# A mixture-of-experts job table: a shorter VectorE chain, work moved to ScalarE and GpSimd, first weights ahead of the gathers, half the filler products

## The reference

```
logits = h @ w_router + b_router
top_vals, top_idx = top_k(logits, 4)             # 32 experts
gates = softmax(top_vals)
for each expert e and each of its tokens t:
    hid = h[t] @ w1[e] + b1[e]                   # 1024 x 2048
    y   = clamped_swiglu(hid) @ w2[e] + b2[e]    # 1024 x 1024
    out[t] += gate * y
```

## Time and profile before

| what | us |
|---|---|
| median of 3 runs (lowest, highest) | 1971.47 (1968.91, 1974.28) |
| the profiled execution | 1971.53 |
| its span, first to last instruction | 1969.7 |
| TensorE busy | 1910.2 (97%) |
| weight loading of TensorE busy | 1398.8 (71%) |
| VectorE / ScalarE / GpSimd busy | 1303.0 / 411.8 / 235.6 |
| mean granted TensorE clock | 0.989 |
| moved by DMA | 498.39 MB, 253 GB/s on the mean |

### The profile page before, as it was taken

One profiled execution on the slowest core, in us unless ns is written; L12 is line 12 of the kernel. 1 busy time (PEld: TensorE's weight loads), 2 busy tenths in 40 slices (PEclk: granted clock), 3 DMA queues, 4 the chain that ended last, 5 costly groups with the idle time before them and its releaser, 6 DMA issues.

```text
span 1969.7 us, 33296 instructions
## 1 busy us (share of the span) xinstructions
PE 1910.2 (97%) x12224; PEld 1398.8 (71%) x12224; DVE 1303.0 (66%) x3759; ACT 411.8 (21%) x910; POOL 235.6 (12%) x317
## 2 busy tenths in 40 slices
PE   7999999997999999999999999999998999999996
PEld 5677777774999999999999999834333444444442
DVE  2787778774377777775666666645355767777665
ACT  1233332222121122222222222223221100001100
POOL 1212222221010111111111111110100000000000
PEclk8999999998999999999999999999999999999998
DMA  9411100113966778788888989999999999999992
GB/s 311 113 43 43 43 18 35 32 33 144 339 207 228 246 261 269 245 282 278 289 285 283 307 300 304 316 368 381 360 368 382 382 375 356 369 369 367 360 360 72
DMA packets 207682, 498.39 MB, mean 253 GB/s; under 512 B 7716, under 2 KB 14928, under 8 KB 200080
## 3 DMA queue, kind: packets, MB, share of 16 engines
q1 hardware_dynamic: 194016, 449.43, 63.7%
q0 software_dynamic: 11312, 39.85, 8.2%
q10 hardware_dynamic: 2304, 8.39, 1.0%
HBM read 470.24 MB, written 27.41 MB: 253 GB/s over the span
## 4 chain that ended last, share of the span: by engine, by line
issue 40%; PE 29%; DMA 5%; POOL 1%; DVE 1%; POOLq 0%; ACT 0%; DVEq 0%; ACTq 0%
PE ps_unit L1885 29%; DMA out_dram<-y_rows,idx_cur 4%; POOL x_got L1378 1%; DMA x_got<-h_rows,idx_next 0%; PE ps_list L1857 0%; POOL carrier L1374 0%; POOL out_dram L1435 0%; POOLq L1096 0%; POOLq L1290 0%; DVE match L1562 0%; DVE reached L1610 0%; POOL out_dram L1390 0%; POOLq L1426 0%; POOLq L1265 0%; DVE xT L1684 0%
## 5 line engine op out<-in xcount | busy, mean ns | idle before, releaser
L1885 PE MATMUL ps_unit<-xT,w_slot 128*128 128x136 f32 (+6 forms) x3840 | 521.5, 298 | 1.6 <-DVE xT L1684 1.6
L1885 PEld LDWEIGHTS ps_unit<-xT,w_slot 128*128 128x128 f32 x3840 | 516.6, 196 | 2.0 <-issue 2.0
L1915 PE MATMUL ps_unit<-w_slot,xT 128*128 128x512 f32 x704 | 306.7, 594 | 0.0
L1279 DVE STREAM_TRANSPOSE xT<-x_got 32x256 f32<-32x256 f32 x644 | 280.5, 436 | 12.1 <-DMA x_got<-h_rows,idx_next 3.7
L1885 PE MATMUL ps_unit<-act_T,w_slot 128*128 128x136 f32 (+6 forms) x1920 | 261.6, 298 | 0.1
L1885 PEld LDWEIGHTS ps_unit<-act_T,w_slot 128*128 128x128 f32 x1920 | 257.9, 190 | 2.2 <-DVE act_T L1659 1.5
L1915 PEld LDWEIGHTS ps_unit<-w_slot,xT 128*128 128x128 f32 x704 | 132.8, 190 | 163.0 <-issue 163.0
L1675 DVE STREAM_TRANSPOSE y_rows<-yT 32x256 f32<-32x256 f32 x372 | 162.1, 436 | 55.0 <-ACT yT L1481 50.1
L928 PE MATMUL ps_c<-hT,w_in_sb 128*128 128x128 f32 x1536 | 182.1, 279 | 4.3 <-DMA w_in_sb<-in_w_in_dram 4.3
L928 PEld LDWEIGHTS ps_c<-hT,w_in_sb 128*128 128x128 f32 x1536 | 177.3, 194 | 9.6 <-DMA w_in_sb<-in_w_in_dram 5.2
L1374 POOL TENSOR_TENSOR carrier<-carrier 128x1 f32<-128x1 f32 x64 | 14.5, 227 | 1319.1 <-issue 610.8
(11 more groups left out here) (294 smaller groups left out, 1790.5 us busy)
## 6 DMA issues: line engine op xcount, KB each, us to landing
w_slot<-in_w_dram SPq DMA_DIRECT2D x192, 2048.0 KB, 12.1
b_row<-in_b_dram SPq DMA_DIRECT2D x11, 1024.0 KB, 12.9
w_in_sb<-in_w_in_dram SPq DMA_DIRECT2D x6, 1024.0 KB, 12.0
b_row<-in_b_dram SPq DMA_DIRECT2D x11, 512.0 KB, 15.1
x_in<-in_x_dram SPq DMA_DIRECT2D x8, 512.0 KB, 3.5
x_res<-in_x_dram SPq DMA_DIRECT2D x8, 512.0 KB, 4.7
out_dram<-x ACTq DMA_DIRECT2D x8, 512.0 KB, 5.1
h_rows<-h ACTq DMA_DIRECT2D x8, 512.0 KB, 3.1
```

Source lines behind the costliest of these rows:

```text
L1279: last = nc.vector.transpose(out[c * Q:(c + 1) * Q, :, tokens], rows.rearrange("p (k c j) -> p k c j", c=P // Q, j=Q)[:, :, c, :])
L1885: last = pe.matmul(ps_unit[p % RING][:, u, 0:n], w, moving[:, k, 0:n], start=(k == 0), stop=(k == KD - 1))
L1915: last = pe.matmul(ps_hid[c], xT[:, k, 0:P], w_slot[:, c, k, :], start=(k == 0), stop=(k == KD - 1))
```

## The change

- VectorE's chain: `counts` is copied first and `rank` later, after the fields. `ended`, `first`, `past` (twice) and `size` are issued without a wait of their own, with independent operations put side by side. The two gate subtracts, the copies of sorted fields and the counts of jobs leave VectorE; it copies one row `ends_f` out of PSUM (a float copy of the ends), which ScalarE converts.
- ScalarE: casts and writes `ends`, `jobs`, `job_row` and `base_row`; it clears `x_got` in four parts after that.
- GpSimd: does the two gate subtracts, the first ahead of its three bias loads, the second behind them, into a buffer `gates_left` of their own; it clears `x_got` no longer and waits for the four parts before the gathers.
- TensorE: ranks and counts go to the bank of `ps_act`, and the five filler products behind them to `ps_list`. The permutation waits for `ends_taken` in place of three table entries. The whole table is awaited ahead of the first list, and four filler products stand between the register loads in place of eight.
- SP: waits for three table entries and the experts' row, loads one register, issues the first piece of weights, waits for both gathers, and issues the other five pieces. The wide loop starts at the second job, and `job_counts` comes behind it.

The declarations of the new buffer and semaphores are left out of the diff.

```diff
         ps_list = ps("ps_list", [P, 512])
         ps_act = ps("ps_act", [P, 4, P])
         ps_x = ps_unit[2:]
+        ps_ranks = ps_act[:].rearrange("p k q -> p (k q)")
...
-        TABLES = 6
+        TABLES = 5
...
 
             sp.wait_ge(pool_moved.sem, 32)
             sp.wait_ge(rows_moved.sem, 16)
-            wide, slim_jobs, narrow_jobs, full = job_counts(sp)
+            sp.wait_ge(experts_read, 1)
+            sp.wait_ge(table_ready, TABLES - 2)
+            wide = sp.value_load(ends[0:1, last_size - 1:last_size], min_val=0, max_val=most_jobs)
             with sp.If(wide > 0):
-                with sp.Fori(0, wide) as q:
+                e = expert_of(sp, 0)
+                load_pieces(0, bass.ds(e, 1))
+                wait(sp, gathered_a, 0)
+                wait(sp, gathered_b, 0)
+                for i in range(1, LOADS):
+                    load_pieces(i, bass.ds(e, 1))
+            with sp.If(wide > 1):
+                with sp.Fori(1, wide) as q:
                     e = expert_of(sp, q)
                     for i in range(LOADS):
                         wait(sp, w_used[i], q - 1)
                         load_pieces(i, bass.ds(e, 1))
+            _, slim_jobs, narrow_jobs, full = job_counts(sp)
             with sp.If(slim_jobs > 0):
                 with sp.Fori(0, slim_jobs) as s:
                     q = s + wide
...
         def _(pool):
+            pool.wait_ge(parts_cast[0], 1)
+            nc.gpsimd.tensor_tensor(gates_left[:], gates[:], gate_parts[:, :, 0, :], ALU.subtract).then_inc(parts_left[0], 1)
             pool.dma_start(y_rows[0:NE, 0, :], b1[0, :, 0:D]).then_inc(pool_moved.sem, 16)
             pool.dma_start(y_rows[0:NE, 1, :], b1[0, :, D:2 * D]).then_inc(rows_moved.sem, 16)
             pool.dma_start(b2_rows[0:NE, :], b2[0]).then_inc(pool_moved.sem, 16)
+            pool.wait_ge(parts_left[0], 1)
+            pool.wait_ge(parts_cast[1], 1)
+            nc.gpsimd.tensor_tensor(gates[:], gates_left[:], gate_parts[:, :, 1, :], ALU.subtract).then_inc(parts_left[1], 1)
             for e in credited:
                 pool.sem_inc(e.sem, e.unit * e.credit)
...
                 nc.gpsimd.memset(digits[:, i:i + 1], float(1 << BITS * i)).then_inc(digits_made, 1)
             nc.gpsimd.memset(carrier[:], 0.0).then_inc(carrier_cleared, 1)
-            nc.gpsimd.memset(x_got[:], 0.0).then_inc(buffers, 1)
             pool.wait_ge(carrier_cleared, 1)
...
-            pool.wait_ge(buffers, 1)
+            pool.wait_ge(buffers, 4)
             wait(pool, idx_ready, 0)
...
         def _(act):
             nc.scalar.copy(gate_parts[:, :, 0, :], gates[:]).then_inc(parts_cast[0], 1)
             nc.scalar.copy(iota_b[:], cst[:, C_IOTA:C_IOTA + CAP]).then_inc(counters_copied, 1)
-            act.wait_ge(parts_left[0], 1)
-            nc.scalar.copy(gate_parts[:, :, 1, :], other[:]).then_inc(parts_cast[1], 1)
             nc.scalar.copy(entry[:, :, 0], cst[:, C_TOK:C_TOK + NB]).then_inc(counters_copied, 1)
             nc.scalar.copy(entry[:, :, 1], cst[:, C_TOK + NB:C_TOK + 2 * NB]).then_inc(counters_copied, 1)
+            act.wait_ge(parts_left[0], 1)
+            nc.scalar.copy(gate_parts[:, :, 1, :], gates_left[:]).then_inc(parts_cast[1], 1)
 
             for bank in ps_flat:
                 nc.scalar.activation(bank, cst[:, 0:2 * CAP], ACT.Copy, scale=0.0).then_inc(units_cleared, 1)
             act.wait_ge(parts_left[1], 1)
             nc.scalar.copy(gate_parts[:, :, 2, :], gates[:]).then_inc(parts_cast[2], 1)
+            act.wait_ge(ends_taken, 1)
+            nc.scalar.copy(ends[:], ends_f[:]).then_inc(table_ready, 1)
+            nc.scalar.activation(jobs[0:1, 1:2], ends_f[0:1, len(SIZES):COLUMNS], ACT.Identity, scale=-1.0,
+                                 bias=last_job[0:1, NE - 1:NE]).then_inc(table_ready, 1)
+            nc.scalar.activation(jobs[0:1, 2:3], ends_f[0:1, last_size - 1:last_size], ACT.Identity, scale=-1.0,
+                                 bias=ends_f[0:1, len(SIZES):COLUMNS]).then_inc(table_ready, 1)
+            act.wait_ge(fields_spread, 1)
+            nc.scalar.copy(job_row[0:1, 0:P], ps_list[0:1, P:2 * P]).then_inc(experts_read, 1)
+            nc.scalar.copy(base_row[:], ps_list[:, 3 * P:4 * P]).then_inc(base_read, 1)
+            nc.scalar.copy(job_row[0:1, P:2 * P], ps_list[0:1, 2 * P:3 * P]).then_inc(table_ready, 1)
+            nc.scalar.copy(jobs[0:1, 0:1], last_job[0:1, NE - 1:NE]).then_inc(table_ready, 1)
+            for h in range(2):
+                for i in range(2):
+                    nc.scalar.activation(x_got[:, h, i * 512:(i + 1) * 512], cst[:, 0:512], ACT.Copy, scale=0.0).then_inc(buffers, 1)
             act.wait_ge(biases_turned, 1)
...
-            dve.wait_ge(parts_cast[0], 1)
-            v.tensor_tensor(other[:], gates[:], gate_parts[:, :, 0, :], ALU.subtract).then_inc(parts_left[0], 1)
...
             dve.wait_ge(ranked, 1)
-            v.tensor_copy(rank[:], ps_list[:, 0:NB * NE].rearrange("p (b e) -> p b e", b=NB))
-            then_wait(v.tensor_copy(counts[:], ps_list[:, NB * NE:NB * NE + NE]))
+            then_wait(v.tensor_copy(counts[:], ps_ranks[:, NB * NE:NB * NE + NE]))
...
                                                  in1=jobs_of[:, i - 2, :], op0=ALU.is_gt, op1=ALU.add))
             over = jobs_of[:, S // CAP - 2, :]
             then_wait(v.tensor_tensor_scan(last_job[:], one_row[:, 0:NE], over, 0.0, ALU.mult, ALU.add))
-            then_wait(v.scalar_tensor_tensor(out=junk_e[:, 0, :], in0=last_job[:], scalar=job, in1=one_row[:, 0:NE],
+            rstep.did(v.scalar_tensor_tensor(out=junk_e[:, 0, :], in0=last_job[:], scalar=job, in1=one_row[:, 0:NE],
                                              op0=ALU.is_le, op1=ALU.mult, accum_out=ended[:]))
             then_wait(v.scalar_tensor_tensor(out=junk_e[:, 1, :], in0=last_job[:], scalar=job, in1=over,
                                              op0=ALU.is_le, op1=ALU.mult, accum_out=started[:]))
-            then_wait(v.tensor_scalar(first[:], started[:], job, -float(CAP), ALU.subtract, ALU.mult))
+            rstep.did(v.tensor_scalar(first[:], started[:], job, -float(CAP), ALU.subtract, ALU.mult))
+            rstep.did(v.tensor_scalar(past[:], ended[:], NE - 0.5, 4096.0, ALU.is_gt, ALU.mult))
             then_wait(v.scalar_tensor_tensor(out=junk_e[:, 2, :], in0=cst[:, C_E:C_E + NE], scalar=ended[:], in1=counts[:],
                                              op0=ALU.is_equal, op1=ALU.mult, accum_out=held[:]))
-            then_wait(v.tensor_scalar(past[:], ended[:], NE - 0.5, 4096.0, ALU.is_gt, ALU.mult))
-            then_wait(v.scalar_tensor_tensor(out=limits[:, 1, :], in0=limits[:, 0, :], scalar=first[:],
+            rstep.did(v.tensor_tensor(past[:], past[:], job, ALU.add))
+            rstep.did(v.scalar_tensor_tensor(out=limits[:, 1, :], in0=limits[:, 0, :], scalar=first[:],
                                              in1=held[:].broadcast_to([P, last_size]), op0=ALU.add, op1=ALU.is_lt,
                                              accum_out=size[:]))
             then_wait(v.scalar_tensor_tensor(out=slim[:], in0=first[:], scalar=float(SLIM), in1=held[:], op0=ALU.add,
                                              op1=ALU.is_ge))
             then_wait(v.scalar_tensor_tensor(out=past[:], in0=slim[:], scalar=-float(P // 2), in1=past[:], op0=ALU.mult,
                                              op1=ALU.add))
-            then_wait(v.tensor_tensor(past[:], past[:], job, ALU.add))
             then_wait(v.scalar_tensor_tensor(out=order_key[:], in0=size[:], scalar=-float(P), in1=past[:],
                                              op0=ALU.mult, op1=ALU.add))
             v.tensor_scalar(reached[:], marks[:], order_key[:], None, ALU.is_gt).then_inc(fields_ready, 1)
@@ -1612,35 +1640,22 @@
             v.tensor_scalar(fields[:, 0:1], ended[:], NE - 1.0, None, ALU.min).then_inc(fields_cast, 1)
             v.tensor_copy(fields[:, 1:2], size[:]).then_inc(fields_cast, 1)
             v.tensor_copy(fields[:, 2:3], first[:]).then_inc(fields_cast, 1)
-            dve.wait_ge(parts_cast[1], 1)
-            v.tensor_tensor(gates[:], other[:], gate_parts[:, :, 1, :], ALU.subtract).then_inc(parts_left[1], 1)
-            dve.wait_ge(parts_left[1], 1)
-            then_wait(v.tensor_tensor(other[:], counts[:].unsqueeze(1).broadcast_to([P, NB, NE]), rank[:], ALU.subtract))
-            then_wait(v.tensor_tensor(other[:], other[:], token[:].unsqueeze(2).broadcast_to([P, NB, NE]), ALU.add))
+            then_wait(v.tensor_copy(rank[:], ps_ranks[:, 0:NB * NE].rearrange("p (b e) -> p b e", b=NB)))
             dve.wait_ge(keys_spread, 1)
             then_wait(v.scalar_tensor_tensor(out=earlier[:], in0=ps_list[:, 2 * P:3 * P], scalar=order_key[:], in1=one_row,
                                              op0=ALU.is_lt, op1=ALU.mult, accum_out=order_rank[:]))
-            v.tensor_copy(ends[:], ps_list[0:1, 3 * P:3 * P + COLUMNS + WORDS]).then_inc(table_ready, 1)
```

(39 more changed lines are left out.)

6 lines of the change are left out of this document (4 added, 2 removed).

## The result

The changed kernel takes 1974.51 us (median of 22 runs, 1969.26 to 1977.71), the kernel before beside it 1969.95 us (22 runs, 1964.89 to 1974.28). The ratio is 1.0020, with a 95% interval of 1.0014 to 1.0027: slower by 0.2%. I had predicted 1965.4 us, in a range that ends at 1969.5; both size and sign were wrong.

What follows compares the result with a forecast made beforehand. The prediction took the first product of the first job to bound the kernel: 1971.5 less 1.6 us (table) and 4.5 us (gathers) gives 1965.4 us, in a range up to 1969.5 us (lower end not given).

Steps and rivals of the forecast that it cites:

- What bounds the kernel: First product of the first job: a microsecond there is a microsecond at the end, as later stages are not edited.
- The chain to the sizes: VectorE, 462 to 466.5 us: 0.64 us from the earlier counts copy, 0.65 from five waits; `reached` starts at about 465.25.
- rival 3: GpSimd's two subtracts lock out VectorE, 0.65 us each; 0.4 to 1 us remain after slack: 1966.2 us, chance 0.10.
- The slack in front of the filler: TensorE's filler before the key product: of VectorE's 2.8 us gain only 1.6 count, 0.9 us is slack.
- The stall at `reached`: VectorE waits on GpSimd's clearing of x_got, costing 1.3 us of a 1.52 us stall; moving it to ScalarE removes this.
- First weights and gathers: SP's queue: first weights issued at 471.0, five pieces after the gathers, second gather landing at 481.35, first product at 484.0.
- Rival 1: Gathers stay slow, set by issue, index reading or scattered rows; only the table counts: 1969.9 us, chance 0.12.
- The term of 4.5 us: Gain at the first product from faster gathers, with fewer weights on the DMA engines beside them.
- rival 2: TensorE not ready: its 6.2 us branch keeps its length, first product only 2.1 us earlier: 1969.4 us, chance 0.16.
- Half the filler: normally nothing.: TensorE's eight passes from 473.75 take 6.8 us, ending at 480.6; at worst 0.35 us late, normally no cost.
- Rival 4: Half the filler leaves TensorE at 1.2 GHz as the wide stage begins; 30 us cold gives 1980 us, chance 0.04.
- The sum: Whole kernel: 1971.5 less 1.6 from the table and 4.5 from the gathers is 1965.4 us, 0.31% less.

Runs made afterwards that it cites:

- run 2: Kernel before with the table part of the change alone, SP's order and the filler left as before: 0.9992 of the kernel before.
- run 6: Kernel before with SP's new order of loads alone (one register load, first weights, both gathers awaited, other five pieces): 0.9997 of the kernel before.
- run 1: Changed kernel with the full filler, eight products between TensorE's register loads in place of four: 0.9978 of the kernel before.
- run 10: Changed kernel with TensorE's register loads ahead of the first token list and the full filler of eight products behind it: 0.9979 of the kernel before.
- run 8: Changed kernel with the full filler and four products left out of the 256-column loop that never runs: 1.0008 of the kernel before.
- run 4: Changed kernel with TensorE's register loads ahead of the first token list and six filler products behind it: 0.9992 of the kernel before.
- run 3: Changed kernel, half filler kept, without TensorE's loop for 256-column jobs, which these data never enter: 0.9978 of the kernel before.
- run 7: Changed kernel, half filler executed, with four filler products added to the 256-column loop that never runs: 0.9995 of the kernel before.

## Why the prediction was wrong, step by step

- **What bounds the kernel** (a microsecond at the first product is one at the end): wrong as a rule for this change. It held for the later stages; but the first job itself could lose time, and did so in two places, 1.75 and 2.95 us. That is the step that gave the wrong sign.
- **The chain to the sizes.** 3.35 us from the rank product to `reached` were forecast, 4.27 came. Of the difference, 0.92, two thirds are rival 3: 0.32 and 0.34 us on the two steps under GpSimd's subtracts. Another 0.27 is on a third step (L1620, 0.25 before, 0.52 after), which ended with an issue of GpSimd's; that this issue held it wasn't tested. The slack in front of the filler took it up, as I had priced it (I called it 0.9; my own 2.8 less 1.6 leaves 1.2): key product at 465.66, which is 4.71 behind the rank product, forecast 4.6. The rule of the Trainium skill ("SBUF — State Buffer", Who interferes with whom) says that whichever of the two engines issues first has the shared ports for its whole instruction; the two rows of 0.50 us, which end with the subtracts, agree.
- **The stall at `reached`** went as forecast, and the table was worth nearly what was said: 1.37 us at the indices where 1.6 was forecast. The 1.59 at the first product of run 2 meets the forecast by luck, with 0.23 of it from the gather.
- **First weights and gathers.** The weights were issued at 8.81 (forecast 9.1). The gathers landed in 5.8 and 5.9 us where 4.5 to 4.8 was forecast and 8.5 to 9.2 had been: three quarters of that gain was there (DMA to landing us, min/median/max):

```profile
DMA to landing us min/median/max: 5.8/5.8/5.9
```

  Rival 1 is out. The term of 4.5 us was nonetheless not there at the first product: SP's order alone gave 1.13 (run 6), and beside the table part it took the first product from 26.59 (run 2) to 24.99 (run 1).
- **The branch, rival 2.** It held, and I gave it 0.16: 6.17 us before, 5.30 after. "Nothing but one piece and the gathers is on the DMA engines now" was true, and the step from there to a short branch failed: these few transfers kept the engines 0.87 busy until the fetch started, and 1.05 in run 10. The fetch itself took 1.04 us before and 1.02 after; the rest is the time until it is started (3.6 and 2.7 us; 3.6 in run 10) and 1.5 us behind it. Whether the fetch waits for the other traffic stays open. For it: at the second branch, where a fetch that came behind the branch found the engines idle (share 0.00), it started after 0.8 to 1.2 us, and in the 13 kernels with the loop, at a share of 0.87 to 1.07, after 1.7 to 3.9. Against it: these are two different branches, and run 8 had 1.7 us at a share of 0.98. No run keeps the engines empty at the first branch. Starting the branch earlier (run 4) or having no loop to jump over (run 3) took it off the path. The Trainium skill ("Runtime: NRT & Kernel Launch", Instruction fetch mechanics) says that a taken branch outside the loaded pages waits for a DMA; the packets of code in the trace agree.
- **"Half the filler: normally nothing."** This failed twice over. I had set its end against the landing of the gathers (it ended at 479.0, before them, as worked out, though the 6.8 us for eight slow passes had no row: ten in 4.54 make 7.3 at half the clock, and they took 5.97, a part of them at 2.4 GHz), but never asked what TensorE's clock does in the pause between filler and transposes when the branch holds it: 1.2 GHz until 491.3, 1.75 us in the first job. Rival 4 had the mechanism and the wrong size: I let it last for 30 us, and it took 10.2. And in this code an edit of the filler moves everything behind it: 2.3 to 3.0 us at a branch 80 us later. No term of mine was for that, although showed that one branch of eleven could take 74 times the median.
- **The sum.** Forecast -6.1. What came: -1.39, +1.75, +2.95. (For rival 2 I had 2.1 earlier at the first product; the transposes at 1.2 GHz, 3.65 us in one row against two of 1.1, are likely the rest: the second half started 1.73 us behind the first, and the first product 3.15 behind it, where I had 1.1 and 2.6.) With the filler left alone it would have been -3.2 at the first product and -0.22% of the time, in the range's upper part.

What stays open beside the wait of the first fetch: why 16 instructions decide whether the fetch starts 1 us ahead of the branch or 1 us behind its start. The runs show that 8 (run 4) and 16 forward make the hole and 0 doesn't; where in between it begins, and what other placements would give, wasn't tried. Nor was it tried to place the loop for 256 columns behind the others.

## What to carry to other kernels

A long branch is a row to price by itself: look at the maximum of a branch's row, not its median, and at when its code is fetched, before counting on what stands behind it. Read the DMA share of just the stretch until that fetch starts; the mean over a longer one can look empty. When an edit takes instructions out of an unrolled program, compare the branches behind it too; padding a part that never runs tells in one run whether placement or work made the difference. Filler that keeps a clock up must reach to the next real work as it will in fact start, not as the data for it arrive.

## What the runs showed of the hardware

- A taken branch over the unused loop took 4.1 to 6.5 us in all 13 kernels that have the loop, in three parts: 1.7 to 3.9 us until the fetch's packet started, 0.89 to 1.05 us for the packet, and 1.53 to 1.58 us from its end to the branch's. Until the fetch started, the DMA engines had a share of 0.87 to 1.07. The kernel without it had no branch over 0.4 us.
- 16 instructions fewer ahead of a branch made it 3.10 to 3.77 us long (four kernels; 3.45 with 8 fewer), where it took 1.04 to 1.38 otherwise, and put a hole of 2.0 to 3.0 us into TensorE's work. In the slow ones the fetch of 16 KB started 0.8 to 1.2 us behind the branch's start, in the others 1.0 to 1.5 us ahead of it.
- A VectorE step of 0.16 to 0.18 us took 0.50 us under a two-input GpSimd subtract of 0.67 to 0.72 us.
- With a pause of 3.86 us between filler and transposes TensorE's clock fell to 1.2 GHz for 10.2 us in the changed kernel; with one of 2.87 us in run 7, for 3.4 us. The first 96 products took 18.9 and 17.1 us.
